# Experts' rows fetched and stored by the DMA queues in place of selection products, and another order of the experts' turns

## The chip, the cores and the metric

One core of a Trainium2 chip runs the whole program once. The metric is the device time of that execution in microseconds (us). PE is TensorE, DVE is VectorE, ACT is ScalarE, POOL is GpSimd, SP is SyncE, whose queue issues the weight loads.

## What is computed

Two blocks of two layers each run over 256 tokens of width 1024, all in float32. The change touches the last half-layer, a mixture of eight SwiGLU experts of which every token uses two:

```python
logits = h @ router_w + router_b                 # 256 x 8
top_vals, top_idx = lax.top_k(logits, 2)
top_w = softmax(top_vals)
combine = sum(one_hot(top_idx, 8) * top_w)       # 256 x 8
y = 0
for e in range(8):
    y = y + combine[:, e:e+1] * ((silu(h @ w_gate[e]) * (h @ w_up[e])) @ w_down[e])
x = x + gate_f * y
return rms_norm(x, final_g)
```

Here h is x normalised, scaled and shifted. An expert's three matrices are 1024 x 3584, 1024 x 3584 and 3584 x 1024.

## The kernel before

The experts stage ends the program. An expert's turn has 14 steps (`ESTEPS`). A step reads 2 MB of gate and up weights (a piece `("gu", s)`) and 1 MB of down weights (`("dn", s)`). SP loads the pieces of all eight turns in one fixed order into 18 units of 1 MB each in SBUF (`LOADS`, `PIECE_AT`); a piece is issued when PE has used what lay in its units (`piece_used`, L775). So at most 18 MB, six steps, are held ahead of PE.

The router's counts decide at run time how wide a turn is (`WIDTHS`, `each_expert`, L619): each engine has one body of code for each width and jumps to it at the head of the turn. In this execution five experts have at most 64 rows (a "few" turn, the body `few(w)`), two have at most 128 (a "full" turn) and one at most 144 (a "wide" turn, `expert_wide`). The wide turn's first step stands apart, in `expert_wide_begin`. Turn 0 is always expert 0; the other seven are sorted by their counts and placed by `RANK_AT`. Before, the turns are few, wide, few, full, few, full, few, few.

What a turn does around its 14 steps:

- **Rows in.** `select` (DVE, L2153) makes the 0/1 matrix `sel` of the next turn's tokens, and PE multiplies the normalised rows `xn` by it: `gather_ahead` (PE, L2935) in three parts at 144 columns, 16 products. ACT (`inputs_ahead`, L1268) and DVE (L2169) scale and shift the result into `hTe`, the next turn's input. This stands at the end of a turn.
- **Rows out.** `by_slot` (PE, L2996) turns the weighted selection `selw`, ACT copies it to `selT`. At the turn's end DVE writes the expert's result rows `ye` (L2228, L2232, L2246), PE multiplies them by `selT` (L3034, L3117), which puts each row at its token's place, and DVE adds the four products to `x` (`add_results`, L2195).

A few turn starts with `gate_up(0)` (L2977), a full turn the same (L2979), the wide one at L3059. A product stands as two records in the trace, a transpose as one. Close to the end of a few or full turn PE runs `gather_ahead(0)`, `turn_hidden(13)`, `gather_ahead(1)`, `down(13)` (L2991, L2993), `gather_ahead(2)` and the scatter L3034.

`addr_align` (L3013, L3093) places two stretches of PE's code at set offsets.

At the program's start SP's first weight load waits for `used[0]`, which POOL gives after its memsets (L864). At the end ACT squares `x`, POOL takes the root (`norm_root_by_rows`), DVE scales and SP stores.

Of the kernel before, what the change touches and what calls it, by code (L numbers as in the profile page):

```python
# [65 lines left out]
AHEAD = WIDTHS[2]  # L66
AHEAD_PARTS = (range(0, 3), range(3, 6), range(6, KD))
# [33 lines left out]
FULL_CLOSE_AT = 74  # L101
WIDE_CLOSE_AT = 16
# [72 lines left out]
RANK_AT = [0] + [(i - 1) // 2 if i % 2 else EXPERTS - 1 - i // 2 for i in range(1, EXPERTS)]  # L175
# [3 lines left out]
def build(nc, t):  # L179
    ctx = ExitStack()  # L180
    with ctx:
# [42 lines left out]
        counts = sb("counts", [P, 2 * EXPERTS], mybir.dt.int32)  # L224

# [127 lines left out]
        selT = ymix[:, 1024:1536].rearrange("p (i s) -> p i s", i=2)  # L353
        ye = rot[:, 2048:4096].rearrange("p (i d) -> p i d", i=2)
# [11 lines left out]
        curp, curw = small[:, 256:258], small[:, 258:260]  # L366
# [88 lines left out]
        route_in = sig("route_in")  # L455
        band_in = sig("band_in")
# [38 lines left out]
        cur_loaded = sig("cur_loaded")  # L495
        sel_ok = sig("sel_ok")
        selw_ok = sig("selw_ok")
# [11 lines left out]
        selT_mm = sig("selT_mm")  # L509
# [8 lines left out]
        stored = sig("stored")  # L518
        out_ok = sig("out_ok")
# [99 lines left out]
        def each_expert(eng, body, begin=None):  # L619
# [7 lines left out]
            with nc.body(f"{name}_head", valid_engines=[eng.engine]):  # L627
# [3 lines left out]
                def run(w, whole=True):  # L631
                    again = eng.mark_branch_hint_location()
                    if whole and begin and w > P:
                        begin(e, w)
                    body(e, w)
                    nc.regs_alu(turn, turn, 1, op=ALU.add)
                    eng.br_lt(turn, EXPERTS, on_true=f"{name}_head", on_false=f"{name}_done{w}").branch_hint(again)
                    with nc.body(f"{name}_done{w}", valid_engines=[eng.engine]):
                        eng.br(f"{name}_end")
# [36 lines left out]
        def few(w):  # L676
            return w == FEW
# [42 lines left out]
        def _(sp):  # L720
# [130 lines left out]
            sp.wait_ge(stored.sem, 16 * NB)  # L851


        @block.gpsimd
        def _(pool):
# [43 lines left out]
            for l in range(DEPTH):  # L899
                norm_root(l * 2)  # L900
                if l == 0:
                    pool.dma_start(route[:], t["route"]).then_inc(route_in.sem, 16)
# [12 lines left out]
            pool.dma_start(rot[:, 2048:4096], t["band"].rearrange("(k p) g s -> p k (g s)", p=P)).then_inc(band_in.sem, 16)  # L915
# [20 lines left out]
            for l in range(DEPTH):  # L936
# [15 lines left out]
                else:  # L952
                    pool.wait_ge(gateB_ok.sem, gateB_ok.at(l, 4))
                    pool.dma_start(finB, t["final_norm_g_2"].partition_broadcast(P)).then_inc(mix_in.sem, 16)
            norm_root_by_rows(U_FIN2)
# [3 lines left out]
        def _(act):  # L959
# [218 lines left out]
            for l in range(DEPTH):  # L1178
# [78 lines left out]
                else:  # L1257
# [10 lines left out]
                    def inputs_ahead(count, bank):  # L1268

                        act.wait_ge(gath_mm.sem, 3 * count - 2)  # L1270
                        for k in AHEAD_PARTS[0]:
                            ins = act.activation(hTe[:, k, 0:AHEAD], bank[:, k * AHEAD:(k + 1) * AHEAD], ACT.Identity, scale=mulc[:, l, 1, k:k + 1], bias=mods[:, l, 3 * KD + k:3 * KD + k + 1])
                        ins.then_inc(hTe_act.sem, 1)
# [18 lines left out]
                    def by_slot(e, w, bank):  # L1292

                        act.wait_ge(selT_mm.sem, e + 1)
                        for i, s0, n in blocks(max(w, P)):
                            ins = act.activation(selT[0:n, i, :], bank[0:n, i * SEQ:(i + 1) * SEQ], ACT.Copy)
                        ins.then_inc(selT_ok.sem, 1)

                    def expert(e, w):

                        last = ESTEPS // 2 - 1
                        if w <= P:
                            act.sem_inc(xTe_act.sem, 1)
                            sigmoids(e, 0, 0, w)
                            by_slot(e, w, T[1])
# [9 lines left out]
                            act.sem_inc(yeT_act.sem, 1)  # L1315
                            return
                        if w > AHEAD:
                            inputs(xgath_mm, e + 1, xTe_act, G[0], AHEAD, w - AHEAD)
                        else:
                            act.sem_inc(xTe_act.sem, 1)  # L1320
# [4 lines left out]
                        by_slot(e, w, S[1])  # L1325
# [7 lines left out]
                        inputs_ahead(e + 2, S[0])  # L1333

                    inputs_ahead(1, G[0])
                    act.wait_ge(counts_ok.sem, 1)
                    each_expert(act, expert)
            act.wait_ge(gath_mm.sem, 3 * (EXPERTS + 1))
            for b in range(NB):
                act.wait_ge(scat_ev.sem, EXPERTS * 4 - 1 + 2 * b)  # L1340
# [4 lines left out]
        def _(dve):  # L1345
# [3 lines left out]
            dve.sem_inc(scat_ev.sem, 1)  # L1349
# [529 lines left out]
            for l in range(DEPTH):  # L1879
# [208 lines left out]
                else:  # L2088
# [4 lines left out]
                    dve.wait_ge(route_in.sem, 16)  # L2093
# [34 lines left out]
                    for b in range(NB):  # L2128
                        ins = dve.tensor_scalar(sel[:, b, :], slots, place[:, b, 0:1], None, ALU.is_equal)
                    ins.then_inc(sel_ok.sem, 1)  # L2130
                    dve.wait_ge(rank_mm.sem, 2)
                    dve.tensor_copy(counts[:, 0:1], S[1][:, 0:1]).then_inc(counts_ok.sem, 1)
                    dve.tensor_copy(curp.unsqueeze(2), place[:, :, 0:1])
                    dve.tensor_copy(curw.unsqueeze(2), weight[:, :, 0:1]).then_inc(cur_loaded.sem, 1)
                    dve.wait_ge(counts_ok.sem, 1)
                    dve.wait_ge(cur_loaded.sem, 1)
# [16 lines left out]
                    def select(e):  # L2153

                        dve.tensor_copy(curp.unsqueeze(2), place[:, :, bass.ds(e, 1)])
                        dve.tensor_copy(curw.unsqueeze(2), weight[:, :, bass.ds(e, 1)]).then_inc(cur_loaded.sem, 1)
                        dve.wait_ge(cur_loaded.sem, e + 1)
                        for b in range(NB):
                            ins = dve.tensor_scalar(sel[:, b, :], slots, curp[:, b:b + 1], None, ALU.is_equal)
                        ins.then_inc(sel_ok.sem, 1)  # L2160

# [7 lines left out]
                    def inputs_ahead(count, part, bank):  # L2169

                        dve.wait_ge(gath_mm.sem, 3 * count - 2 + part)
                        for i, k in enumerate(AHEAD_PARTS[part]):
                            ins = dve.tensor_scalar(hTe[:, k, 0:AHEAD], bank[:, i * AHEAD:(i + 1) * AHEAD], mulc[:, l, 1, k:k + 1], mods[:, l, 3 * KD + k:3 * KD + k + 1], ALU.mult, ALU.add)
                        if part == 2:
                            ins.then_inc(hTe_dve.sem, 1)
# [19 lines left out]
                    def add_results(e, banks):  # L2195

                        dve.wait_ge(scat_ev.sem, e * 4 + 1)
                        for b in range(NB):
                            for half in range(2):
                                j = 2 * b + half  # L2200
                                xs = x[:, b, half * 512:(half + 1) * 512]
                                dve.wait_ge(scat_mm.sem, e * 4 + (j + 1))
                                dve.tensor_tensor(xs, banks[j][:, :], xs, ALU.add).then_inc(scat_ev.sem, 1)

                    def expert(e, w):

                        if w > AHEAD:
                            inputs(xgath_mm, e + 1, xTe_dve, G[1], AHEAD, w - AHEAD)
                        else:
                            dve.sem_inc(xTe_dve.sem, 1)  # L2210

                        n = FEW if few(w) else P * len(blocks(w))
                        for b in range(NB):
                            for c0 in range(0, max(n, P), n):
                                ins = dve.tensor_scalar(selw[:, b, c0:c0 + n], slots[:, 0:n], curp[:, b:b + 1], curw[:, b:b + 1], ALU.is_equal, ALU.mult)
                        ins.then_inc(selw_ok.sem, 1)
                        dve.wait_ge(sel_ok.sem, e + 1)
                        dve.wait_ge(selw_ok.sem, e + 1)
                        select(e + 1)
# [3 lines left out]
                        if w <= P:  # L2223
                            inputs_ahead(e + 2, 1, G[1])
                            dve.wait_ge(down_mm.sem, e * ESTEPS + (FSTEPS + ESTEPS))
                            dve.sem_inc(yeT_dve.sem, 1)
                            if few(w):
# [6 lines left out]
                            inputs_ahead(e + 2, 2, T[1])  # L2234
                            return add_results(e, SCAT)
# [6 lines left out]
                        dve.wait_ge(ye_mm.sem, e + 1)  # L2242
                        for i, s0, n in blocks(w):
# [4 lines left out]
                        inputs_ahead(e + 2, 1, S[1])  # L2248
                        inputs_ahead(e + 2, 2, T[0])
                        add_results(e, G)  # L2250

                    inputs_ahead(1, 1, G[1])
                    inputs_ahead(1, 2, T[1])
                    each_expert(dve, expert)
            dve.wait_ge(scat_ev.sem, EXPERTS * 4 + 1)
# [8 lines left out]
        def _(pe):  # L2264
# [395 lines left out]
            for l in range(DEPTH):  # L2660
# [78 lines left out]
                pe.wait_ge(band_in.sem, 16)  # L2739
# [163 lines left out]
                else:  # L2903
                    pe.wait_ge(route_in.sem, 16)
# [22 lines left out]
                    def gather_wide(w):  # L2927

                        for k in range(KD):
                            for b in range(NB):  # L2930
                                ins = mm(G[k // KH][:, k % KH * P:k % KH * P + w - AHEAD], xn[:, b, k * P:(k + 1) * P], sel[:, b, AHEAD:w], start=(b == 0), stop=(b == NB - 1))
                            if k % KH == KH - 1:
                                ins.then_inc(xgath_mm.sem, 1)

                    def gather_ahead(part, bank):  # L2935
# [320 lines left out]
```

## Time and profile before

| | |
|---|---|
| median of 3 runs | 2415.78 us (2414.87 to 2418.22) |
| the profiled execution | 2413.9 us, span 2412.0 us |
| PE busy | 2370.4 us, 98% of the span |
| DVE, ACT, POOL busy | 935.5, 365.1, 55.4 us |
| chain of work that ended last | PE 92%, DMA 3%, DVE 3% of the span |
| experts stage, first product to the end of the span | 1463.69 to 2412.0 us |
| DMA over the span | 617.59 MB, mean 256 GB/s |

Times of the trace count from the start of the span. The profiled execution's own time is 1.9 us above its span. A busy PE here means that a product is in it, which says nothing of how far it is from its peak.

### The profile page before, as it was taken

How to read it: one execution, taken by the hardware profiler on the slowest of the kernel's cores; microseconds unless marked ns; L12 is line 12 of the kernel's file. 1: busy time of each engine (PE TensorE's matmuls, PEld its weight loads, DVE VectorE, ACT ScalarE, POOL GpSimd, SP SyncE). 2: the span in 40 equal slices, each digit the busy share in tenths (PEclk: the TensorE clock that was granted, in tenths of full speed). 3: DMA queues.
4: the chain of work that ended last, by engine and by line, in shares of the span. 5: the costliest groups of instructions: out<-in, count | busy, mean ns of one | idle time of the engine just before them, and what ended most of it. 6: DMA issues, size and time to landing. Idle time of an engine off the chain costs nothing.

```text
span 2412.0 us, 30124 instructions
## 1 busy us (share of the span) xinstructions
PE 2370.4 (98%) x12002; PEld 1579.7 (65%) x12003; DVE 935.5 (39%) x1962; ACT 365.1 (15%) x988; POOL 55.4 (2%) x110
## 2 busy tenths in 40 slices
PE   9999999999999999999999999999999999999997
PEld 8956476669665666676778756699854455445554
DVE  4565233255563356755687462100211021102111
ACT  2254010012351100011000112100111011101111
POOL 0000000000000000000000000000000000000000
PEclk9999999999999999999999999999999999999999
DMA  7432343444322677554577469974899689968997
GB/s 275 151 113 97 113 170 144 148 180 162 131 78 101 263 299 298 197 199 182 237 297 314 167 234 392 425 292 175 361 417 426 243 343 426 425 270 346 425 426 301
DMA packets 78989, 617.59 MB, mean 256 GB/s; under 512 B 5984, under 2 KB 6112, under 8 KB 39184
## 3 DMA queue, kind: packets, MB, share of 16 engines
q1 hardware_dynamic: 73920, 558.39, 58.3%
q0 software_dynamic: 4656, 56.47, 5.6%
q8 instruction: 98, 1.61, 0.3%
q10 hardware_dynamic: 288, 0.90, 0.1%
q14 instruction: 27, 0.22, 0.0%
HBM read 614.69 MB, written 1.05 MB: 255 GB/s over the span
## 4 chain that ended last, share of the span: by engine, by line
PE 92%; DMA 3%; DVE 3%; ACT 1%; issue 1%; SPq 0%; POOL 0%; DVEq 0%; POOLq 0%; ACTq 0%
PE S L2977 9%; PE T L2597 9%; PE S L2979 8%; PE G L2336 6%; PE G L2613 5%; PE G L2991 4%; PE G L2993 4%; PE G L2368 3%; PE G L2551 3%; PE G L2876 3%; DMA big<-in_moe_pack 3%; PE S L2857 3%; PE T L3045 2%; PE G L2679 2%; PE G L2563 2%; PE G L3072 2%
## 5 line engine op out<-in xcount | busy, mean ns | idle before, releaser
L2191 DVE TENSOR_TENSOR turns<-S,turns 128x128 f32<-128x128 f32 (+2 forms) x105 | 35.5, 338 | 657.4 <-ACT turns L1285 657.4
L2977 PE MATMUL S<-big,hT 128*64 128x256 f32 x2240 | 271.4, 385 | 10.6 <-DMA big<-in_moe_pack 10.5
L2977 PEld LDWEIGHTS S<-big,hT 128*64 128x64 f32 x2240 | 156.9, 138 | 119.1 <-issue 37.0
L2597 PE MATMUL T<-hT,big 128*128 128x256 f32 x960 | 217.2, 379 | 1.1 <-ACT big L1173 1.1
L2597 PEld LDWEIGHTS T<-hT,big 128*128 128x128 f32 x960 | 182.2, 190 | 49.4 <-issue 27.7
L2979 PE MATMUL S<-big,hT 128*128 128x512 f32 x448 | 201.3, 593 | 0.4 <-issue 0.4
L2979 PEld LDWEIGHTS S<-big,hT 128*128 128x128 f32 x448 | 82.8, 190 | 94.8 <-issue 94.8
L2368 PE MATMUL G<-big,hT 128*128 128x384 f32 x320 | 109.0, 490 | 0.8 <-ACT big L1063 0.8
L1290 ACT ACTIVATE pT<-T 128x128 f32<-128x128 f32 (+1 forms) x98 | 30.2, 308 | 521.8 <-PE T L2956 521.8
L2336 PE MATMUL G<-big 128*128 128x186 f32 (+1 forms) x536 | 91.8, 322 | 0.0
L2336 PEld LDWEIGHTS G<-big 128*128 128x128 f32 x536 | 86.6, 190 | 0.2
L2368 PEld LDWEIGHTS G<-big,hT 128*128 128x128 f32 x320 | 59.3, 190 | 40.2 <-issue 4.8
L2991 PE MATMUL G<-big,pT 128*64 128x512 f32 x360 | 84.9, 592 | 0.0
L2551 PE MATMUL G<-big,yT 128*128 128x512 f32 x192 | 83.1, 592 | 0.0
L1794 DVE TENSOR_TENSOR big<-big 128x256 f32<-128x256 f32 x64 | 25.8, 422 | 138.3 <-ACT big L1173 138.2
L2876 PE MATMUL G<-big,pT 128*128 128x512 f32 x176 | 77.4, 593 | 0.8 <-DVE pT L2006 0.7
L1173 ACT ACTIVATE big<-T 128x256 f32<-128x256 f32 x60 | 23.0, 383 | 337.9 <-PE T L2597 337.9
L1424 DVE CUSTOM_DVE_ANT_0 big<-big 128x1024 f32<-128x1024 f32 x64 | 74.1, 1220 | 0.0
L1285 ACT ACTIVATE turns<-S 128x128 f32<-128x128 f32 (+2 forms) x105 | 33.0, 314 | 222.4 <-PE S L2977 93.3
L2551 PEld LDWEIGHTS G<-big,yT 128*128 128x128 f32 x192 | 36.2, 190 | 44.0 <-issue 44.0
L2993 PE MATMUL G<-big,pT 128*128 128x512 f32 x144 | 64.7, 592 | 0.0
L3045 PE MATMUL T<-hT,big 128*128 128x144 f32 x448 | 58.0, 292 | 2.9 <-issue 2.9
(500 smaller groups left out, 3475.5 us busy)
## 6 DMA issues: line engine op xcount, KB each, us to landing
big<-in_moe_pack SPq DMA_DIRECT2D x112, 2048.0 KB, 15.2
big<-in_moe_pack SPq DMA_DIRECT2D x72, 1024.0 KB, 12.4
big<-in_w_ff SPq DMA_DIRECT2D x32, 2048.0 KB, 8.4
big<-in_ada_pack POOLq DMA_DIRECT2D x24, 2048.0 KB, 12.1
big<-in_ffn_pack SPq DMA_DIRECT2D x11, 3072.0 KB, 12.6
big<-in_gate_pack SPq DMA_DIRECT2D x16, 1536.0 KB, 6.4
consts<-in_moe_pack SPq DMA_DIRECT2D x24, 1024.0 KB, 14.3
big<-in_proj_pack SPq DMA_DIRECT2D x15, 1488.0 KB, 6.4
```

What stands on the lines that cost most here:

```text
L1424: ins = dve.tensor_tensor_reduce(row, row, condrow, 1.0, 0.0, ALU.mult, ALU.add, mods[:, a, col:col + 1])
L2336: ins = mm(out, left[:, k, :], right[:, k, :], start=(k == 0 and i not in (2, 3)), stop=(k == KH - 1), skip_group_check=True)
L2368: ins = mm(G[b if n < 4 else 1][:, 0:GATE_N], hT[:, k, b * P:(b + 1) * P], w[:, k, :], start=(k == 0), stop=(k == KD - 1))
L2551: ins = mm(G[j][:, :], yT[:, 4 * n + k, b * P:(b + 1) * P], w[:, k, half * 512:(half + 1) * 512], start=(k == 0), stop=(k == 3))
L2597: ins = mm(up_bank(c, f), w[:, k, f * P:(f + 1) * P], hT[:, k, :], start=(k == 0), stop=(k == KD - 1))
L2613: ins = mm(P7[i][:, :], left[:, f, :], right[:, f, :], start=(c == 0 and f == 0), stop=(c == 7 and f == 1))
L2876: return mm(G[j][:, :], ffhid[:, n % 2, f, b * P:(b + 1) * P], dn[:, f, half * 512:(half + 1) * 512], start=(n == 0 and f == 0), stop=(n = ...
L2977: ins = mm(S[s % 2][f * FEW:(f + 1) * FEW, 0:SEQ], hTe[:, k, 0:FEW], wt[:, k, f * SEQ:(f + 1) * SEQ], start=(k == 0), stop=(k == KD - 1))
L2979: ins = mm(S[s % 2][:, :], hTe[:, k, 0:P], wt[:, k, :], start=(k == 0), stop=(k == KD - 1))
L2991: ins = mm(G[2][half * FEW:(half + 1) * FEW, :], ehid[:, s % 2, f * FEW:(f + 1) * FEW], wt[:, f, half * 512:(half + 1) * 512], start=first ...
L2993: ins = mm(G[2 + half][:, :], ehid[:, s % 2, f * P:(f + 1) * P], wt[:, f, half * 512:(half + 1) * 512], start=first, stop=last)
L3045: ins = mm(H4[2 * (s % 2) + piece][:, f * w:(f + 1) * w], wt[:, k, c0:c0 + P], hTe[:, k, 0:w], start=(k == 0), stop=(k == KD - 1))
```

## The change

Rows in: POOL writes `xn` to a store in DRAM (`row_store`), makes for each turn a list of its tokens in DRAM (four scatters of 128 numbers each), loads the lists (`where`), and fetches for each turn two blocks of up to 128 rows by indirect transfers into `xe`. PE turns a block by eight transposes (`turn_ahead`, `turn_wide`). Only turn 0 is still gathered by products (`gather_first`), at 128 columns. `hTe` ahead of a turn now holds 128 columns, so the wide turn (144) turns its second block in `expert_wide_begin`.

Rows out: a turn's `ye` is stored to `results` in DRAM by two DMAs that ACT issues (`store_results`). Only the last turn still has `by_slot`, the scatter products and `add_results`, now behind the loop (`closing`). During the last turn POOL fetches, for the two token blocks, the earlier and the later result row of each token (four indirect transfers, one after the other), multiplies each by its weight and adds it to `x`.

Further: `results` (8 MB) is filled once, by a POOL DMA in layer 0 of the first block; POOL fills `token_list` ahead of `used[0]`; `RANK_AT` is reversed, which makes the turns few, few, wide, few, full, few, full, few; the two `addr_align` go, one comes at the end of a loop body.

```diff
-AHEAD_PARTS = (range(0, 3), range(3, 6), range(6, KD))
+AHEAD_PARTS = (range(0, KD // 2), range(KD // 2, KD))
-RANK_AT = [0] + [(i - 1) // 2 if i % 2 else EXPERTS - 1 - i // 2 for i in range(1, EXPERTS)]
+RANK_AT = [0] + [TURNS - 1 - (i - 1) // 2 if i % 2 else i // 2 - 1 for i in range(1, EXPERTS)]
...
+            pool.iota(token[:], pattern=[[P, NB]], base=0, channel_multiplier=1)
+            step.do(pool.memset(where[:], 0))
+            pool.dma_start(token_list.rearrange("(p j) o -> p (j o)", p=P), where[:]).then_inc(lists_in.sem, 16)
             for i in range(NSLOT):
                 pool.sem_inc(used[i].sem, 1)
...
+                if l == 0:
+                    pool.wait_ge(consts_in.sem, 16)
+                    pool.dma_start(results.rearrange("s e i (h d) -> s (e i h) d", h=2), vecs[:, V_N - 512:V_N].unsqueeze(1).broadcast_to([P, 2 * LIST, 512])).then_inc(rows_moved.sem, 16)
...
+            def rows_of_turn(e, i):
+                if e + i > 1:
+                    pool.wait_ge(xe_in[i].sem, 16 * (e + i - 1))
+                pool.indirect_dma_start(xe[:, i, :], None, row_store, bass.IndirectOffsetOnAxis(ap=where[:, 2 * e + i:2 * e + i + 1], axis=0)).then_inc(xe_in[i].sem, 16)
...
+            pool.dma_start(row_store.rearrange("(b p) d -> p b d", p=P), xn).then_inc(rows_moved.sem, 16)
+            turn_lists()
+            pool.wait_ge(gath_mm.sem, 2)
+            pool.wait_ge(rows_moved.sem, 48)
+            pool.wait_ge(lists_in.sem, 32 + 64 + 16)
+            rows_of_turn(0, 1)
+            rows_of_turn(1, 0)
+            shares()
+            pool.wait_ge(xgath_mm.sem, 2)
+            rows_of_turn(1, 1)
+            for e in range(2, EXPERTS):
+                pool.wait_ge(gath_mm.sem, 2 * e)
+                rows_of_turn(e, 0)
+                pool.wait_ge(xgath_mm.sem, 2 * e)
+                rows_of_turn(e, 1)
...
+            pool.wait_ge(ye_out.sem, 32 * EXPERTS)
+            rows = results.rearrange("s e i d -> (s e i) d")
+            for n, (b, i) in enumerate(((0, 0), (0, 1), (1, 0), (1, 1))):
+                pool.indirect_dma_start(xe[:, 1, :], None, rows, bass.IndirectOffsetOnAxis(ap=found[:, 2 + i, b:b + 1], axis=0)).then_inc(rows_moved.sem, 16)
+                pool.wait_ge(rows_moved.sem, 16 * (n + 4))
+                w = (w_early, w_late)[i][:, b:b + 1]
+                step.do(pool.tensor_scalar(xe[:, 1, :], xe[:, 1, :], w, None, ALU.mult))
+                ins = pool.tensor_tensor(x[:, b, :], x[:, b, :], xe[:, 1, :], ALU.add)
...
+                    def store_results(e, w):
+                        act.wait_ge(ye_dve.sem, e * 2 + 4)
+                        for i in range(2):
...
+                            act.dma_start(out.rearrange("s e d -> s (e d)"), src).then_inc(ye_out.sem, 16)
...
+                    def turn_ahead(part, bank):
+                        for i, k in enumerate(AHEAD_PARTS[part]):
+                            ins = pe.transpose(bank[:, i * P:(i + 1) * P], xe[:, 0, k * P:(k + 1) * P], ident[:])
+                        ins.then_inc(gath_mm.sem, 1)
...
                         gate_up(e, 0, w)
-                        pe.wait_ge(scat_ev.sem, e * 4 + 1)
-                        by_slot(e, w, T[1])
+                        pe.wait_ge(ye_dve.sem, e * 2 + 2)
                         for s in range(1, ESTEPS):
-                            if s == ESTEPS - 1 and not few(w):
-                                pe.addr_align(FETCHED, offset=FULL_CLOSE_AT, max_nops=0)
                             gate_up(e, s, w)
                             down(e, s - 1, w)
-                        pe.wait_ge(sel_ok.sem, e + 2)
-                        gather_ahead(0, G[0])
+                        pe.wait_ge(xe_in[0].sem, (e + 1) * 16)
+                        turn_ahead(0, G[0])
                         turn_hidden(e, ESTEPS - 1, w)
-                        gather_ahead(1, G[1])
+                        turn_ahead(1, G[1])
                         down(e, ESTEPS - 1, w)
-                        pe.wait_ge(selT_ok.sem, e + 1)
-                        gather_ahead(2, T[1])
```

## Rows read from the trace of the kernel before

**Rows 1.** Windows by turn: stretch, length, busy of each engine, PEclk, DMA share, GB/s.
```profile
1463.70:1550.60 86.90, 84.95 (x617) 45.69 (x617) 16.05 (x50) 10.57 (x34) 0.00 (x0) 1.00 0.98 403
1550.60:1736.50 185.90, 182.97 (x1426) 176.23 (x1426) 21.05 (x47) 17.25 (x28) 0.00 (x0) 0.99 0.73 290
...
1821.60:1977.50 155.90, 155.36 (x408) 71.94 (x408) 20.03 (x47) 13.37 (x33) 0.00 (x0) 1.00 0.80 323
...
2218.50:2303.40 84.90, 84.90 (x619) 45.67 (x620) 14.06 (x45) 10.52 (x33) 0.00 (x0) 1.00 1.01 426
```

**Rows 2.** Windows in the first few turn, columns as in Rows 1.
```profile
1484.00:1550.60 66.60, 64.65 (x464) 34.55 (x460) 11.10 (x31) 8.19 (x25) 0.00 (x0) 1.00 1.01 425
```

**Rows 3.** Timeline, the last turn's last two steps: start, length, engine, line, work.
```profile
2388.81 2.81 PE L2977 MATMUL S<-big,hT 128*64 128x256 f32 x24 [1.58 <-DMA big<-in_moe_pack]
...
2397.79 1.94 PE L2991 MATMUL G<-consts,pT 128*64 128x512 f32 x8
```

**Rows 4.** Timeline, boundary of two few turns.
```profile
2295.11 1.74 PE L2939 MATMUL G<-yT,rot 128*128 128x144 f32 x12
...
2296.99 0.28 ACT L1290 ACTIVATE pT<-T 128x128 f32<-128x128 f32 x1 [3.21 <-PE T L2956]
2297.16 1.19 ACT L1272 ACTIVATE hT<-G,mods,misc 128x144 f32<-128x144 f32 x3
...
2298.36 1.94 PE L2991 MATMUL G<-consts,pT 128*64 128x512 f32 x8
...
2303.32 3.67 PE L2977 MATMUL S<-big,hT 128*64 128x256 f32 x32
```

**Rows 5.** Timeline, the wide turn: its second step, its end, the turn behind it.
```profile
1563.27 8.79 PE L3045 MATMUL T<-hT,big 128*128 128x144 f32 x56 [2.93 <-issue]
...
1720.86 0.73 PE L3096 MATMUL G<-zcol,consts 128*128 128x2 f32 x6
...
1723.55 1.06 PE L3107 MATMUL T<-consts,hT 128*128 128x128 f32 x8
...
1725.53 1.29 DVE L2246 TENSOR_TENSOR rot<-T,o 128x512 f32<-128x512 f32 x2 [3.30 <-PE G L3107]
...
1736.48 3.67 PE L2977 MATMUL S<-big,hT 128*64 128x256 f32 x32
```

**Rows 6.** Timeline, boundary of a full and a few turn.
```profile
1965.58 1.63 PE L2939 MATMUL G<-yT,rot 128*128 128x144 f32 x12
...
1968.74 3.60 PE L2993 MATMUL G<-consts,pT 128*128 128x512 f32 x8
...
1977.46 3.67 PE L2977 MATMUL S<-big,hT 128*64 128x256 f32 x32
```

**Rows 7.** Timeline, start of the program.
```profile
1.18 0.42 SPq L724 DMA_DIRECT2D big<-in_proj_pack  x1
...
7.91 6.49 PE L2296 MATMUL G<-big,hT 128*128 128x372 f32 x20 [0.16 <-DMA big<-in_proj_pack]
```

**Rows 8.** Timeline of POOL: a DMA's issue and two small operations.
```profile
18.95 0.71 POOL L902 DMA_DIRECT2D route<-in_route  x1
...
113.25 0.23 POOL L874 TENSOR_TENSOR small<-small,epsc 128x20 f32<-128x20 f32 x1
...
1441.70 0.19 POOL L874 TENSOR_TENSOR small<-small,epsc 128x1 f32<-128x1 f32 x1 [14.47 <-ACT pT L969]
```

**Rows 9.** A window in layer 0 of the first block, columns as in Rows 1.
```profile
340.00:360.00 20.00, 20.00 (x75) 13.86 (x74) 4.15 (x7) 1.15 (x3) 0.00 (x0) 1.00 0.44 161
```

**Rows 10.** Timeline, the gather of turn 0 and its first products.
```profile
1458.00 4.61 PE L2939 MATMUL G<-yT,rot 128*128 128x144 f32 x24
...
1463.69 3.67 PE L2977 MATMUL S<-big,hT 128*64 128x256 f32 x32
```

**Rows 11.** DMA issues, 1390 to 1463 us: size, median us from issue to landing.
```profile
yT<-in_final_norm_g POOLq DMA_DIRECT2D x1, 512.0 KB, 11.4
```

**Rows 12.** DMA issues, 2290 to 2412 us.
```profile
big<-in_moe_pack SPq DMA_DIRECT2D x11, 2048.0 KB, 32.3
```

More of the change, by code:

```diff
@@ L100 @@
 FETCHED = 256
[L101 to L102 removed]
+REST_AT = 100
 KH = KD // 2
@@ L518, in build @@
         stored = sig("stored")
+        xe_in = [sig(f"xe_in{i}") for i in range(2)]
+        ye_out = sig("ye_out")
         out_ok = sig("out_ok")
@@ L638, in run @@
                     with nc.body(f"{name}_done{w}", valid_engines=[eng.engine]):
+                        if closing:
+                            closing(w)
+                        if begin and w == P:
+                            eng.addr_align(FETCHED, offset=REST_AT, max_nops=0)
                         eng.br(f"{name}_end")
@@ L1290, in hidden_turned, with by_slot @@
                         act.activation(ehid[:, i, 0:n], T[0][:, i * SEQ:i * SEQ + n], ACT.Copy).then_inc(eh_ok.sem, 1)
[L1292 to L1296, printed above, removed]
-                        ins.then_inc(selT_ok.sem, 1)
+                    def by_slot(w):
+                        act.wait_ge(scat_mm.sem, 1)
+                        if few(w):
+                            ins = act.activation(selTN, T[1][:, 0:SEQ], ACT.Copy)
+                        else:
+                            for i, s0, n in blocks(w):
+                                ins = act.activation(selT[0:n, i, :], (T[1] if w <= P else G[0])[0:n, i * SEQ:(i + 1) * SEQ], ACT.Copy)
+                        ins.then_inc(selT_ok.sem, 1)
+                    def store_results(e, w):
+                        act.wait_ge(ye_dve.sem, e * 2 + 4)
+                        for i in range(2):
+                            h = slice(i * 512, (i + 1) * 512)
+                            if few(w):
+                                out, src = results[0:FEW, bass.ds(e, 1), 0, h], ye[i * FEW:(i + 1) * FEW, 0, 0:512]
+                            elif w <= P:
+                                out, src = results[:, bass.ds(e, 1), 0, h], ye[:, 0, h]
+                            else:
+                                n = blocks(w)[i][2]
+                                out, src = results[0:n, bass.ds(e, 1), i, :], ye[0:n, i, :]
+                            act.dma_start(out.rearrange("s e d -> s (e d)"), src).then_inc(ye_out.sem, 16)
                     def expert(e, w):
@@ L3098, in expert_wide @@
                         pe.sem_inc(eh_turned.sem, ESTEPS)
[L3099 to L3102 removed]
+                        pe.wait_ge(xe_in[0].sem, (e + 1) * 16)
+                        turn_ahead(0, S[0])
                         pe.wait_ge(yeT_act.sem, e + 1)
@@ L3108, in expert_wide @@
                         ins.then_inc(ye_mm.sem, 1)
[L3109 to L3118 removed]
+                        turn_ahead(1, S[1])
                     def any_expert(e, w):
```

267 lines of the change are left out of this document (155 added, 112 removed).

## The prediction

> **What bounds the kernel now.** I first cut the experts stage into its turns [rows 1]. PE is busy through each turn, so every record that leaves PE shortens a turn unless the weights are late. The GB/s column says when they are: a few turn draws 403 to 426 GB/s with a DMA share near 1, a full or wide one 290 to 323. A turn reads 42 MB of weights. At 425 GB/s [rows 2] a unit of 1 MB (1.049e6 bytes) takes 2.47 us and a turn's 42 units 103.6 us. A few turn is shorter than that and lives on the 18 units held ahead; full and wide turns fill them again. Two few turns in a row outrun the loads: in the last turn PE waits for weights, 1.58 us before step 13 [rows 3], and its last `down` ends at 2399.73, 96.4 us into the turn against 81.8 us one turn earlier [rows 3, 4]. So 14.6 us of the last pair is weights. Then I read what PE does between the last steps of a turn and the first products of the next [rows 4 to 6], because the change removes most of it.
>
> **The change part by part.** All sums are against the profiled execution (span 2412.0, time 2413.9), 1.9 below the median 2415.78.
>
> *Start.* SP's first load, issued at 1.18, is what PE's first product waits for [rows 7]. POOL now runs an iota, a memset and a DMA issue ahead of its release. The issue is 0.71, small operations about 0.2 each [rows 8], with their waits **+1.3** (0.9 to 2.5; the iota isn't in the trace, the nearest row is 0.2).
>
> *Filling `results`.* 8.4 MB in layer 0 of the first block. There DMA moves 161 GB/s [rows 9], so 264 are free and it takes 32 us under products that wait for nothing: 0. With no cover it would be 8.4/0.425 = 20 us.
>
> *Turn 0's gather.* 32 records at 128 columns for 32 at 144 (5.7 us to the first product [rows 10]): **-0.7**.
>
> *A few turn's boundary.* From `gather_ahead(0)` to the next `gate_up(0)`: 2295.11 to 2303.32, 8.2 us [rows 4]. After: four transposes 0.5 (eight are 1.06 [rows 5]), `turn_hidden` 0.3, four transposes 0.5, 0.1 for ACT's copy (0.28), `down` 1.94. ACT's four scalings (three are 1.19) and VectorE's four end under `down`. The jump to the next body, which the scatter products covered, gets 0.4 more. In all 3.7, saved 4.5; with the two transposes and the wait of `by_slot` in step 1 (0.5) **-5.0** a turn. Queued behind the new wait for `xe_in` is all of PE; rows are asked for a whole turn ahead, so I charge nothing. For turn 1 they come last: lists by some 28 small POOL operations (0.3 each with their waits, 8 us), then three DMA rounds of 0.7 plus 11.4 each [rows 8, 11]; begun at about turn 0's first product, that ends near 1508, and they are due some 75 us into the turn, near 1540. If they were late by 20 us, it would cost nothing either, since that turn pair waits for weights.
>
> *A full turn's boundary.* 1965.58 to 1977.46, 11.9 [rows 6], becomes 0.5 + 0.3 + 0.5 + 0.3 + 3.6 = 5.2; with `by_slot` **-7.1** a turn.
>
> *The wide turn's.* 1720.86 to 1736.48, 15.6 [rows 5]. After: 0.7, 0.5, a wait of 0.9 for the copies, sixteen transposes 2.1, four more 0.5, then VectorE's four `ye` operations (1.29 for two) and four scalings before the second half of `gate_up(0)`, 2.4 net. In all 7.1, **-8.5**. At its start `turn_wide` (1.1) and a second block of scalings, behind ACT's stores, come new: **+4.0**.
>
> *ACT's stores.* Two issues a turn, 0.4 each by the nearest row [rows 7], between `ye` and the first sigmoid, 3.7 us after the turn's start [rows 4]: hidden, with 1 us to spare beside the table load. Each further us would move PE by as much, a turn.
>
> *The order.* The pair of few turns now stands at the front. Weights decide it again. From the pair's start to its last `gate_up` took 2388.81 - 2218.5 = 170.3. The first pair begins with all 18 units landed; I credit one unit, -2.5. New traffic shares the stretch: five blocks of 0.5 MB, turn 0's results (0.26 MB), lists, the tail of `row_store`: 2.9 MB at 425 GB/s is 6.8, with small pieces **+8** (5 to 28: at the upper end each block holds the loads for half of its 11.4). So 175.8, then step 13 and the boundary, 10.9 before and 9.1 after. The saved boundaries of these two turns are lost to the weights. Behind the pair the wide turn refills all units, and no other pair is left.
>
> *Tail.* ACT now copies the turned selection after the last turn's two stores, and PE waits for it: **+3.0** (1 to 6).
>
> The sum, first product to last `down`. Before: 1463.7 to 2399.7, 936.0. After: pair 184.9, wide start 4.0, wide 177.4, few 79.9, full 148.8, few 79.9, full 148.8, last few 79.5, in all 903.2. That is -32.8; with +1.3, -0.7 and +3.0, **-29.2**: 2384.7 for the profiled execution, 2386.6 on the median's scale. I say **2386**.
>
> *The results' fetch* hides under the last few turn and has little cover to spare. It begins when turn 6's stores have landed (0.9 + 0.8 + 11.4 = 13.1). Four times a fetch (0.7 + 11.4) and two POOL operations on 1024 columns follow; by the slope of 20 columns against one [rows 8], 2.1 ns a column, that is 2.3 each. 13.1 + 4 x 16.7 = 80. It is due at 79.5 + 3.4 = 83. I take 0, the last fetches being quicker once the weights have landed. Lower end 0; upper end 32.3 a fetch, the big pieces' landing in the last turns [rows 12]: 13.1 + 4 x 37.6 = 163, 80 late.
>
> The Trainium skill ("DMA: Bandwidth & Descriptors", section "Anatomy of one DMA — SWDGE (gpsimd) path") gives such a DMA about 2.0 us plus its bytes at 436 GB/s, an estimate of 3.2 for half a MB. The row of 11.4, taken while the weights ran at full rate, differs. By the page the chain would end at 47 and the late cases below would fall away; the sum would stay.
>
> **The rivals.**
>
> *The pair costs more.* The new transfers slow the weights beyond their bytes. For it: 11.4 for half a MB. Against it: the traffic kept its 425 GB/s [rows 2]. At the upper end +20, 2406.
>
> *Code late at the boundaries.* The wide turn's second step began after 2.93 us in which PE waited for nothing that the profile shows, behind a jump [rows 5]. The `addr_align` go, every body moves, and the products that covered the jump are gone. At all seven boundaries that is 20: 2406. Against it: the few and full boundaries of before show no such gap [rows 4, 6].
>
> *The results' fetch is late, and still faster.* Landings of 12 to 19 us: 2387 to 2414. A rule puts a mechanism of its own here: POOL held while VectorE works. VectorE is busy 14.06 us of a few turn [rows 1]; if POOL lost all of it in the last turn, the chain would end at 94, 11 late: 2397. The Trainium skill ("SBUF — State Buffer", section "SBUF: two separate sides") states it as an exclusive lock on a shared port that keeps POOL from writing descriptors. The trace of before can't show it, since POOL does nothing during the turns [rows 1].
>
> *Slower.* The same four fetches, one behind the other: each us of landing counts four times. The change loses from 11.4 + (3 + 29)/4 = 19.4 us a fetch on; at 32.3 the program ends at 2386 + 80 = 2466. For it: the fetches run against weights that land after 32. Against it: they are of another queue, and the one POOL row is 11.4.
>
> **How the numbers follow.** Within 0.2% (5 us) a measurement of this kernel can't be told from no change. Forecast 0.52 (own range 2372 to 2396); pair dearer 0.09; code late 0.11; fetch late but faster 0.14, the lock 0.04 of it; fetch late and slower 0.10; all gains lost to several of these, no change, 0.04. So faster 0.86, same 0.04, slower 0.10. The range takes the forecast's lower end with its smallest costs (start 0.9, pair 5, tail 1, jumps 0: 2386 - 0.4 - 3 - 2 - 3, and a fuller start of the pair, 8 more), 2368, up to 2412, which leaves out the slower case and the far end of the late one: **2368 to 2412**.
>
> **What would show it.** Right: few turns near 80 and full ones near 149 us in the windows by turn; the waits for `moe_pack` in the second turn, none in the last; no scatter products but four at the end; POOL's last addition to `x` before the last `down`. Wrong: PE or VectorE waiting for POOL at the end; gaps of 2 to 3 us in front of the first `gate_up`; ACT's sigmoid late behind its DMA issues; first products later than 1464.3; PE waiting for `xe` at the end of turn 0 beyond what the weights would have cost.

## The result, and the profile after

The changed kernel takes 2401.9 us (median of 5 runs, 2400.4 to 2404.3) against 2415.8 before (median of 5): a ratio of 0.994, 95% interval 0.9929 to 0.9951. It is 13.9 us faster, where 29.8 were forecast: inside the range of 2368 to 2412, with half of the gain. The profiled execution has a span of 2398.6 us, where the forecast's sum gives 2412.0 - 29.2 = 2382.8.

The windows by turn answer to [rows 1]; the turns are now few, few, wide, few, full, few, full, few. Columns: stretch, its length, busy time of PE, its weight load, DVE, ACT and POOL with their instructions, PEclk, DMA share, GB/s. The third line is the wide turn; the stretch above it also holds the wide turn's start, and the last one ends with the last `down`.

```profile
1463.90:1543.70 79.80, 79.27 (x583) 41.72 (x582) 11.10 (x37) 10.31 (x33) 19.06 (x45) 1.00 1.01 416
1543.70:1654.50 110.80, 87.29 (x591) 46.90 (x591) 11.61 (x38) 13.08 (x39) 2.61 (x3) 0.95 1.01 426
1654.50:1826.80 172.30, 170.43 (x1382) 169.96 (x1382) 15.19 (x32) 16.84 (x27) 0.94 (x1) 0.99 0.77 312
1826.80:1908.30 81.50, 79.75 (x583) 41.97 (x583) 12.12 (x39) 10.43 (x33) 2.20 (x3) 1.00 1.01 424
1908.30:2057.00 148.70, 148.57 (x374) 67.04 (x374) 13.35 (x33) 13.40 (x33) 2.48 (x3) 1.00 0.88 362
2057.00:2145.70 88.70, 81.97 (x583) 43.89 (x583) 11.37 (x35) 10.43 (x33) 1.24 (x2) 0.98 1.01 425
2145.70:2294.40 148.70, 148.57 (x372) 67.07 (x372) 13.41 (x33) 13.40 (x33) 1.23 (x2) 1.00 0.87 360
2294.40:2383.50 89.10, 81.91 (x584) 43.58 (x584) 10.82 (x34) 10.44 (x33) 24.82 (x12) 0.98 0.95 397
```

Beside the forecast's own terms:

| stretch | forecast | measured | difference |
|---|---|---|---|
| first few pair, to its last `down` (1648.07) | 184.9 | 184.2 | -0.7 |
| wide start (to 1654.49) | 4.0 | 6.4 | +2.4 |
| wide turn | 177.4 | 172.3 | -5.1 |
| few turn 3 | 79.9 | 81.5 | +1.6 |
| full turn 4 | 148.8 | 148.7 | -0.1 |
| few turn 5 | 79.9 | 88.7 | +8.8 |
| full turn 6 | 148.8 | 148.7 | -0.1 |
| few turn 7, to its last `down` | 79.5 | 89.1 | +9.6 |
| sum | 903.2 | 919.6 | +16.4 |

The program reaches the first product 0.4 earlier than forecast (1463.9) and its tail is 0.2 shorter (2383.5 to 2398.6, 15.1). So the missing 16 us lie in the turns: turns 5 and 7 lost 18.4, and the other stretches together gained 2.0. Turn 0 took 79.8 us with the same work; turns 5 and 7 took 9 us more each. The chain of what ended last, and the waits of PE over the experts stage (us in total, times, longest), say to what:

```profile
PE 87%; DMA 7%; DVE 3%; ACT 1%; SPq 1%; issue 1%; ACTq 0%; POOL 0%; DVEq 0%; POOLq 0%
```

```profile
PE S L3095 <- DMA big<-in_moe_pack: 31.9, 18, 4.2
PE S L3188 <- ACT hT L1386: 5.1, 1, 5.1
PE G L3154 <- ACT yT L1417: 2.6, 1, 2.6
PE S L3097 <- DMA big<-in_moe_pack: 1.8, 2, 0.9
```

Before, the chain had 3% of DMA, and PE's waits for `moe_pack` were 10.5 us, all in the last pair. Now they are 33.7 us. Why a few turn behind a full one waits at all, though a full turn has time to refill the units, is seen on SP's queue. This is its timeline in full turn 4 (start, length, queue and line, tile; a group reaches from its first to its last issue), and the windows there, columns as above:

```profile
1975.24 21.95 SPq L787 DMA_DIRECT2D big<-in_moe_pack  x5
1997.45 0.33 SPq L787 DMA_DIRECT2D turns<-in_moe_pack  x1
2020.78 0.33 SPq L787 DMA_DIRECT2D consts<-in_moe_pack  x1
2027.86 21.36 SPq L787 DMA_DIRECT2D big<-in_moe_pack  x10
```

```profile
2000.00:2010.00 10.00, 10.00 (x26) 4.45 (x26) 0.85 (x2) 0.77 (x2) 0.00 (x0) 1.00 0.78 332
2010.00:2020.00 10.00, 10.00 (x26) 4.45 (x25) 0.85 (x2) 0.77 (x2) 0.00 (x0) 1.00 0.00 0
2020.00:2030.00 10.00, 10.00 (x26) 4.54 (x25) 0.85 (x2) 0.77 (x2) 0.00 (x0) 1.00 0.44 134
2030.00:2040.00 10.00, 10.00 (x26) 4.54 (x25) 0.85 (x2) 0.77 (x2) 0.00 (x0) 1.00 1.00 403
```

SP's waits for PE in that stretch, 1990 to 2050 (us in total, times, longest):

```profile
SPq L787 <- PE G L3111: 27.9, 3, 22.7
SPq L787 <- PE S L3097: 23.9, 4, 6.6
```

The loads stand in one queue. The piece `("dn", 13)` (in `consts`, unit 16) may be loaded only when PE has used `("dn", 9)`, which lies in the same unit. SP waits 22.7 us for that (for L3111, the full turn's `down`), and DMA moves nothing from 2010 to 2020. The next turn's `("gu", 0)` stands behind it, and it has a wait of its own: its units 0 and 1 hold `("gu", 11)` until PE has used that (L3097, the full turn's `gate_up`), 6.6 us more. So two places set the restart, and a free place for `("dn", 13)` alone would not have moved it. `("gu", 0)` goes out at 2027.86, 29.2 us before the full turn ends. At 425 GB/s 11.8 units can land in that time, where the forecast had all 18 full. From there DMA is busy throughout (share 1.00, 416 GB/s) to the end of turn 5, 117.8 us after that load. PE's last wait for weights in turn 5 ends at 2135.93. Up to there DMA moved 414 GB/s for 108.1 us, 42.7 units: the turn's pieces up to that one are 40, the new transfers of the stretch 1.5, and later pieces were under way. In turn 7 it is the same: 2265.31 to 2383.48, 118.2.

The kernel before had the same standstill. SP's timeline of before, full turn 3, not among the rows ahead of the prediction:

```profile
1934.36 0.33 SPq L773 DMA_DIRECT2D consts<-in_moe_pack  x1
1941.44 21.36 SPq L773 DMA_DIRECT2D big<-in_moe_pack  x10
```

There the load of `("gu", 0)` came 36.0 us before the full turn's end (1977.46), and the few turn behind it ended at 2062.60, 121.2 us after the load, without a wait. The change takes 7.1 off the full turn's end and 5.0 off the few turn. Both lie inside this stretch: 121.2 - 12.1 = 109.1 was what the forecast asked for, 117.8 is what it took with the weights as the limit. The difference, 8.7, is what turn 5 lost.

### The profile page after: what moved, and what is told of

Read it like the earlier page. It is cut to its first block, busy times and chain, and to the rows that moved or that the text cites. A ratio compares the mean times of both kernels' runs of the same rounds, so it can differ in the third digit from the quotient of the medians.

```text
span 2398.6 us, 29590 instructions
## 1 busy us (share of the span) xinstructions
PE 2327.4 (97%) x11738; PEld 1550.4 (65%) x11739; DVE 899.8 (38%) x1869; ACT 367.8 (15%) x994; POOL 115.7 (5%) x194
## 4 chain that ended last, share of the span: by engine, by line
PE 87%; DMA 7%; DVE 3%; ACT 1%; SPq 1%; issue 1%; ACTq 0%; POOL 0%; DVEq 0%; POOLq 0%
PE T L2710 9%; PE S L3097 8%; PE S L3095 7%; DMA big<-in_moe_pack 7%; PE G L2449 6%; PE G L2726 5%; PE G L3111 4%; PE G L2481 4%; PE G L2664 3%; PE G L3109 3%; PE G L2989 3%; PE S L2970 3%; PE G L2792 2%; PE T L3174 2%; PE G L2676 2%; PE G L3201 2%
## 5 line engine op out<-in xcount | busy, mean ns | idle before, releaser
L3095 PE MATMUL S<-big,hT 128*64 128x256 f32 x2240 | 276.5, 391 | 34.0 <-DMA big<-in_moe_pack 31.9
L3095 PEld LDWEIGHTS S<-big,hT 128*64 128x64 f32 x2240 | 163.1, 140 | 144.1 <-issue 65.4
L3097 PE MATMUL S<-big,hT 128*128 128x512 f32 x448 | 201.0, 593 | 1.8 <-DMA big<-in_moe_pack 1.8
L3097 PEld LDWEIGHTS S<-big,hT 128*128 128x128 f32 x448 | 82.9, 190 | 97.3 <-issue 93.7
L3111 PE MATMUL G<-big,pT 128*128 128x512 f32 x144 | 64.7, 592 | 0.0
L2989 PEld LDWEIGHTS G<-big,pT 128*128 128x128 f32 x176 | 32.7, 190 | 38.7 <-issue 37.3
```

Of the source, the lines that this page charges most:

```text
L2989: return mm(G[j][:, :], ffhid[:, n % 2, f, b * P:(b + 1) * P], dn[:, f, half * 512:(half + 1) * 512], start=(n == 0 and f == 0), stop=(n = ...
L3095: ins = mm(S[s % 2][f * FEW:(f + 1) * FEW, 0:SEQ], hTe[:, k, 0:FEW], wt[:, k, f * SEQ:(f + 1) * SEQ], start=(k == 0), stop=(k == KD - 1))
L3097: ins = mm(S[s % 2][:, :], hTe[:, k, 0:P], wt[:, k, :], start=(k == 0), stop=(k == KD - 1))
L3111: ins = mm(G[2 + half][:, :], ehid[:, s % 2, f * P:(f + 1) * P], wt[:, f, half * 512:(half + 1) * 512], start=first, stop=last)
```

## Experiments

Three theories, as the expectations number them. Theory 1: the place of the pieces makes the loads restart late, and the few turns behind a full turn are bound by weights. Theory 2: the new transfers on the queues of POOL and ACT slow the weights beyond their bytes. Theory 3: the new order of the turns is what costs. The first four kernels ran beside runs of before with a median of 2416.3 us, the other four beside 2416.6.

### The same kernel, other places for the later pieces

The first twelve pieces stay; thirteen of the others move to units that come free earlier. `("dn", 13)` now has to wait for `("dn", 4)` in place of `("dn", 9)`, and the next turn's `("gu", 0)` for `("gu", 6)` in place of `("gu", 11)`.

```diff
-GU_AT = (0, 2, 5, 8, 11, 14, 0, 2, 6, 8, 11, 0, 4, 14)
-DN_AT = (4, 7, 10, 13, 16, 17, 5, 10, 13, 16, 2, 7, 17, 16)
+GU_AT = (0, 2, 5, 8, 11, 14, 0, 3, 8, 12, 6, 4, 8, 13)
+DN_AT = (4, 7, 10, 13, 16, 17, 2, 10, 15, 11, 17, 10, 15, 16)
```

> The changed kernel, with only the places of the later weight pieces in the 18 units changed, so that no load has to wait for a piece that is used late while other units are free. Theory 1 (the few turns behind a full turn are bound by weights, because the loads stand still 15 to 17 us in each full turn and start again too late): the waits for weights of turns 3, 5 and 7 go (1.6 + 8.7 + 9.5 = 19.8 us above the forecast), the first pair costs some 2 us more; 2384 us, 2380 to 2389; turns 5 and 7 take 80 to 81 us and 80 to 81 us. Theory 2 (the new small transfers on the POOL and ACT queues slow the weights beside them): the bytes and their places in time are nearly the same, so 2398 to 2404 us, turn 5 over 86 us. Theory 3 (the new order of the turns costs it): no change, 2399 to 2405 us.

Measured: 2383.3 us (2381.9 to 2385.7), ratio to before 0.9862 (0.9847 to 0.9877). Its windows for turns 3, 4, 5 and 7, and SP's timeline in full turn 4:

```profile
1828.30:1908.70 80.40, 79.51 (x583) 41.65 (x583) 11.97 (x39) 10.45 (x33) 2.08 (x3) 1.00 1.00 411
1908.70:2057.40 148.70, 148.57 (x372) 67.05 (x372) 13.51 (x33) 13.44 (x33) 2.61 (x3) 1.00 0.91 376
2057.40:2137.50 80.10, 79.32 (x584) 41.77 (x583) 11.26 (x35) 10.46 (x33) 1.08 (x2) 1.00 1.01 422
...
2286.20:2366.40 80.20, 79.56 (x584) 42.09 (x584) 10.81 (x34) 10.46 (x33) 24.88 (x12) 1.00 0.94 394
```

```profile
1996.72 14.29 SPq L787 DMA_DIRECT2D big<-in_moe_pack  x4
2011.32 0.33 SPq L787 DMA_DIRECT2D consts<-in_moe_pack  x1
2012.01 41.08 SPq L787 DMA_DIRECT2D big<-in_moe_pack  x10
```

`("gu", 0)` now goes out at 2012.01, 45.4 us ahead of the full turn's end in place of 29.2, and the few turns take the forecast's 80. Theory 1 holds with its number, and this is the fastest kernel here that computes everything. All transfers, their bytes and the order of the turns are as they were, so theories 2 and 3 are not needed for these 18.6 us. The edit moves more than the restart; that the restart is what counts is read from SP's timeline, and from DMA, which in the changed kernel had no pause left in turn 5 that another place could have filled. The pair at the front waits as before: 185.1 us to its last `down`.

### Most of the new transfers taken away

```diff
-                rows_of_turn(e, 1)
+                if e == 2:
+                    rows_of_turn(e, 1)
+                else:
+                    pool.wait_ge(xe_in[1].sem, 16 * e)
+                    pool.dma_start(xe[0:1, 1, 0:SEQ], row_store[0:1, 0:SEQ]).then_inc(xe_in[1].sem, 16)
...
-                            act.dma_start(out.rearrange("s e d -> s (e d)"), src).then_inc(ye_out.sem, 16)
+                            act.dma_start(out.rearrange("s e d -> s (e d)")[0:1], src[0:1]).then_inc(ye_out.sem, 16)
```

> The changed kernel without most of its new transfers: each turn's result stores carry one row instead of all, and the second block of rows is fetched in the turns 0, 1 and 2 alone, with one row of 1 KB in its place in the others (so the output lacks the results of the turns before the last). Some 0.75 MB less in a few turn and 1 MB in a full one. Theory 1 (weights, bytes alone): at 425 GB/s 2.3 us off each of turns 5 and 7, 1.6 off turn 3, 2 to 3.5 off the first pair; 2392 us, 2388 to 2397. Theory 2 (the transfers slow the weights beyond their bytes): the waits of turns 3, 5 and 7 go altogether, some 20 us, and more of the pair's; 2376 to 2384 us. Theory 3 (the order): within 3 us of 2402.

Measured: 2394.3 us (2393.5 to 2395.6), ratio 0.9908 (0.9892 to 0.9923); inside theory 1's range, far from theory 2's. Turn 5:

```profile
2054.10:2139.00 84.90, 79.98 (x583) 42.41 (x582) 11.36 (x35) 10.44 (x33) 1.21 (x2) 1.00 1.01 426
```

It is 3.8 us shorter than in the changed kernel and still 4.8 longer than with the new places. A full turn's results (0.5 MB) and one second block of rows (0.5 MB) are gone from the stretch that binds it, 2.5 us at 425 GB/s; 2.3 was expected. PE's busy time fell by 2.0 (81.97 to 79.98): some products of turn 5 that ran slowly in the changed kernel (last section) do not here. Turn 7 gained only 0.4. In its stretch no row block is fetched in either kernel, so only turn 6's results are gone: 1.2 us by their bytes, not the 2.3 expected. So the new transfers cost about their bytes, and not the 20 us of theory 2.

### The order alone, and the rows alone

The kernel before with the new `RANK_AT`:

```diff
-RANK_AT = [0] + [(i - 1) // 2 if i % 2 else EXPERTS - 1 - i // 2 for i in range(1, EXPERTS)]
+RANK_AT = [0] + [TURNS - 1 - (i - 1) // 2 if i % 2 else i // 2 - 1 for i in range(1, EXPERTS)]
```

> The kernel before with the new order of the turns and nothing else. Theory 1: in the kernel before a few turn takes 85 us, just longer than the weights behind a full turn need, so the order moves only the pair from the end to the start; the end pair's 10.5 us of waits for weights go, 5 to 10 come back in turn 1; 2411 us, 2407 to 2416. Theory 2: the same, there are no new transfers. Theory 3 (the order costs 15 us or more in itself): 2425 to 2435 us.

The changed kernel with the line of before (the same diff the other way round):

> The changed kernel with the order of the turns of the kernel before (few, wide, few, full, few, full, few, few). Theory 1: the few turns behind the full ones wait for weights as they do now, and the last few turn, the second of a pair at the end, waits 15 to 25 us; 2408 us, 2403 to 2415. Theory 3 (the order takes what the rows gain): 2384 to 2392 us. Theory 2 says the same as theory 1 within its bounds.

Measured: the order alone 2412.4 us, ratio 0.9986 (0.9977 to 0.9995); the rows alone 2404.2, ratio 0.9947 (0.9934 to 0.9961). With the order alone the pair takes 178.0 us to its last `down`, against 181.3 at the end of the kernel before, and few turns 3 and 5 keep 85.1. Rows alone, the turns 4, 6 and 7 (windows):

```profile
1953.00:2040.70 87.70, 80.36 (x583) 42.83 (x582) 11.35 (x35) 10.44 (x33) 1.16 (x2) 1.00 1.01 424
...
2189.40:2278.50 89.10, 80.43 (x583) 42.83 (x582) 11.34 (x35) 10.44 (x33) 0.59 (x1) 1.00 1.01 424
2278.50:2386.70 108.20, 87.77 (x583) 46.66 (x584) 9.69 (x33) 10.44 (x33) 24.81 (x12) 0.94 0.94 397
```

The few turns behind a full one are as long as in the changed kernel, whatever the order. Theory 3 falls: the order gains some 2 to 4 us in either kernel and loses none. Both times lie inside theory 1's ranges.

### The new places in the kernel before, and with the old order

The diff of the first experiment, on the kernel before and on the kernel "rows alone":

> The kernel before with the same new places of the weight pieces and nothing else. Theory 1 (the limit behind a full turn lies just under the 85 us that a few turn takes in the kernel before, and the change went below it): turns 4 and 6 of this kernel wait for nothing and gain nothing, only the pair at the end gains, by up to 6 us; 2411 us, 2407 to 2417. Rival (the places were poor in any case, and the 18 us have nothing to do with the change): 2394 to 2400 us.

> The changed kernel with the new places of the weight pieces and with the order of the turns of the kernel before. Theory 1 (the order only moves the pair): turns 2, 4 and 6 at 80 to 81 us, and the pair at the end waits as long as the one at the start, some 25 us, with the 2 MB of the last fetches beside it up to 5 more; 2386 us, 2381 to 2391. Theory 3 (the order itself costs): 2365 to 2375 us.

Measured: on before 2413.7 us, ratio 0.999 (0.9981 to 0.9999); with the rows and the old order 2386.2, ratio 0.9871 (0.9856 to 0.9886). So the same two lines are worth 0.1% in the kernel before and 0.8% in the changed one. That is 2.9 us before (2416.6 to 2413.7) and 18.6 after. In the kernel before, a few turn behind a full one takes 85.1 us with either map: the restart was early enough for it. The end pair gained less than the 6 us allowed for (180.8 in place of 181.3). With the old order the few turn behind a full one is 80.4 us, and the pair at the end waits as expected:

```profile
2181.10:2261.50 80.40, 79.50 (x583) 41.96 (x582) 11.35 (x35) 10.45 (x33) 0.59 (x1) 1.00 1.01 424
2261.50:2369.70 108.20, 86.78 (x583) 46.30 (x583) 9.69 (x33) 10.46 (x33) 24.83 (x12) 0.95 0.94 397
```

### Half of the down weights left where they are

```diff
-                c0, n = (0, 2 * UNIT) if kind == "gu" else (2 * UNIT, UNIT)
-                sp.dma_start(unit_rows(LOADS[m]), t["moe_pack"][e, s][:, c0:c0 + n]).then_inc(arrival(PIECES.index(LOADS[m]))[0], 16)
+                c0, n = (0, 2 * UNIT) if kind == "gu" else (2 * UNIT, UNIT // 2)
+                sp.dma_start(unit_rows(LOADS[m])[:, 0:n], t["moe_pack"][e, s][:, c0:c0 + n]).then_inc(arrival(PIECES.index(LOADS[m]))[0], 16)
```

> The changed kernel with only the first half of each down piece loaded from the second expert on (half of the down weights are old ones, so the output differs): 35 MB a turn in place of 42. Theory 1: no turn waits for weights, also not the first pair; the 33.7 us of such waits go and nothing comes in their place; 2368 us, 2364 to 2373, every few turn near 80 us. Rival (a few turn cannot take 80 us behind a full one for another reason, POOL's fetches or the row transposes): turns 5 and 7 stay over 84 us, 2376 us or more.

Measured: 2360.1 us (2359.8 to 2360.9), ratio 0.9764 (0.9749 to 0.9779). Turn 1 with the wide start, turns 5 and 7:

```profile
1543.60:1633.10 89.50, 81.70 (x590) 44.07 (x590) 11.63 (x38) 13.07 (x39) 2.61 (x3) 0.99 1.01 421
...
2035.80:2115.90 80.10, 79.34 (x584) 41.75 (x583) 11.26 (x35) 10.45 (x33) 1.16 (x2) 1.00 1.01 419
...
2264.60:2343.90 79.30, 79.28 (x584) 41.83 (x584) 10.83 (x34) 10.45 (x33) 24.84 (x12) 1.00 0.86 357
```

The rows, the transposes and the fetches are all there, and a few turn takes 80 us: nothing but weights kept it longer. The time is below the expected range (2364 to 2373): the gain of 41.8 is 8 us above the 33.7 of waits, so the expectation, which had nothing beside the waits, was too small. From the first product to the last `down` it is 880.4 in place of 919.6. PE's waits for weights fell by 31.2 (2.5 are left), and its busy time by 877.75 - 868.30 = 9.5 with the same products: some had run slowly behind the waits. The last section shows one.

### Without the results' stores

This is for the 5.1 us at the wide turn's start, where PE waits for ACT.

```diff
-                            act.dma_start(out.rearrange("s e d -> s (e d)"), src).then_inc(ye_out.sem, 16)
+                            act.sem_inc(ye_out.sem, 16)
```

> The changed kernel without the results' stores: ACT raises the semaphore in their place (so the output lacks the results of the turns before the last). This is for the 5.1 us that PE waits at the wide turn's start. Theory 1 (ACT's two DMA issues and the code around them stand ahead of the scalings of the wide turn's second block): the wait falls to 1 to 2 us. Rival (the jump to the wide body and the table load cost it): it stays over 4 us. In all, with the stores' bytes gone too, 2395 us by the first (2391 to 2398), 2398 by the rival.

Measured: 2394.1 us (2391.9 to 2395.2), ratio 0.9902 (0.9887 to 0.9917); but the wait is still 4.0 us. First the changed kernel, then this one (timeline, ACT and PE at the wide start):

```profile
1649.24 1.17 ACTq L1435 DMA_DIRECT2D results<-rot  x2
...
1651.83 1.28 ACT L1386 ACT_TABLE_LOAD   x1 [4.45 <-issue]
1653.12 1.13 ACT L1386 ACTIVATE hT<-G,mods,misc 128x16 f32<-128x16 f32 x4
```

```profile
1648.21 1.09 PE L3056 MATMUL G<-consts,rot 128*128 128x128 f32 x8 [0.27 <-issue]
...
1650.65 1.28 ACT L1386 ACT_TABLE_LOAD   x1 [3.40 <-issue]
1651.95 1.13 ACT L1386 ACTIVATE hT<-G,mods,misc 128x16 f32<-128x16 f32 x4
...
1653.32 2.12 PE L3188 MATMUL S<-hT,big 128*128 128x144 f32 x8 [4.02 <-ACT hT L1386]
```

The stores cost 1.1 us there, so my theory fell, and the wait agrees with the rival (it stays over 4 us). The total does not part the two (2395 and 2398 were expected): the stores' bytes are gone as well. The rows show what PE's 4.0 us are made of. PE's `turn_wide` (L3056) ends at 1649.30; then come 1.35 us in which ACT waits for nothing that the profile shows, a table load of 1.28 and the scalings. They are not the wide body's own: in the changed kernel 1.3 to 1.4 us lie between ACT's DMA issues and the table load at the few and full boundaries too, where PE does not wait for them. What fills them stays open, so the jump is not shown as a cause.

## Why the prediction was right and wrong

**Wrong: the weights behind a full turn.** The step that failed is "full and wide turns fill them again", and on it "Behind the pair the wide turn refills all units, and no other pair is left", with its sums of 79.9 and 79.5 for turns 3, 5 and 7, which put the wait for weights behind a full turn at nothing. It took the mean rate of a full turn, 323 GB/s [rows 1], as a sign that the 18 units are full at its end. They are not: 29.2 us of loads are some 12 units. The loads stand still, for two places in the buffer, and restart at a set point of the turn. From there a few turn behind it ended 117.8 and 118.2 us after `("gu", 0)` went out, with DMA busy (shares 1.00 and 0.95). The kernel before used 121.2, so 3.4 of the 12.1 us saved in each full turn and the few turn behind it could be kept. Twice 8.7 is 17.4 of the loss; turns 5 and 7 show 18.4, the last with the fetches' 2 MB beside its weights. Turn 3, behind the wide turn, lost 1.6 (80.4 with the new places). Against the forecast the three turns lost 20.0 us; the first experiment gives 18.6 of it back by moving the restart, and the same edit gives 2.9 before the change. Loading half of the down weights takes the wait away too. That cause is shown.

**Right in its size: the boundaries.** Full turns 148.7 for 148.8; turn 0 79.8 for 79.9. Where weights don't bind, a few turn takes 79.3 to 80.4. The row transposes cost PE what was charged, and it nowhere waits for rows.

**Right: the pair.** 184.2 for 184.9. The 8 us of new traffic and 2.5 of credit were both estimates, and the runs bear both out. The order alone, without new traffic, took 178.0 where the pair at the end took 181.3: a credit of 3.3. From 178.0 to 184.2, with the last step and boundary 2.0 shorter (8.9 for 10.9), the traffic cost 8.2. Half the down weights show that some 21 us of its length (turn 1: 104.4 to 83.2 to the last `down`) is weights, the slow products behind the waits included.

**Right in sum: start, gather and tail.** First product 1463.9 for 1464.3, but in part by luck: the program's first weight product began 0.4 us later and not 1.3 (8.33 for 7.91, outside the 0.9 to 2.5), and turn 0's gather took 0.3 less and not 0.7. Tail 15.1 for 15.3. In the tail PE waits 2.6 us for ACT, behind ACT's two DMA issues (1.18); without stores that wait is 1.4.

**Off in both directions: the wide turn.** Its start took 6.4 for 4.0 (no table load and none of ACT's time ahead of it were charged). The turn itself took 13.6 off for 8.5: its boundary went from 15.6 [rows 5] to 5.5 (1821.27 to 1826.77), 1.6 more than forecast, the gap of 2.93 in its second step [rows 5] did not return, and 0.6 more is not traced.

**The rivals.** Three of them would have given times near the measured one, and none is what happened. The pair was not dearer. No few or full boundary shows code late by 2 to 3 us; they show 0.5 at most. ACT's open 1.3 to 1.4 us may be of that kind; PE pays for them at the wide boundary alone. One sign of being wrong did show: in turn 5 ACT's first sigmoid began 5.2 us into the turn and not 3.7 (2062.19), behind its DMA issues, those open 1.3 us and the table load, but PE did not wait for it. The results' fetch was hidden: this is POOL's first and last round in turn 7, and PE's last `down`.

```profile
2310.45 1.00 POOL L1066 DMA_INDIRECT rot<-results,idx  x1 [18.87 <-DMA results<-rot]
2322.61 2.85 POOL L1069 TENSOR_SCALAR rot<-rot,small 128x1024 f32<-128x1024 f32 x1 [11.17 <-DMA rot<-results,idx]
...
2359.29 1.01 POOL L1066 DMA_INDIRECT rot<-results,idx  x1 [0.27 <-POOL x L1070]
2368.81 2.84 POOL L1069 TENSOR_SCALAR rot<-rot,small 128x1024 f32<-128x1024 f32 x1 [8.51 <-DMA rot<-results,idx]
2371.74 2.35 POOL L1070 TENSOR_TENSOR x<-x,rot 128x1024 f32<-128x1024 f32 x1
...
2381.54 1.94 PE L3109 MATMUL G<-consts,pT 128*64 128x512 f32 x8
```

The chain ends at 2374.1, 9.4 us before the last `down` and 79.7 into the turn, where the sum of its terms gave 80. VectorE was busy for 10.8 us of this turn. POOL lost nothing of that size: its two operations took 2.8 and 2.4 us in each of the four rounds. With the new places of the weights the last turn is shorter, and the spare falls to 1.6 us (POOL ends at 2364.7, the last `down` at 2366.4). A longer fetch chain was not tried, so what a late one would cost is untested. (The lower end of the range is 2369.6 by its own terms; 2368 stands there.)

## What to carry to other kernels

When loads stand in one ordered queue in front of a buffer, read from the queue's own timeline where they last stood still, and take the time from that restart to the end of the work it feeds as a floor; a mean rate below the maximum does not say that the buffer is full. All savings that lie between one restart and that end share the same few us of spare, so they are not to be added turn by turn. Places in the buffer that cost next to nothing (0.1% before) can be the bound after a change that makes the work shorter (0.8%), so the map is to be looked at again after it.

## What the runs showed of the hardware

A wait for weights can cost PE more than its length. In turn 5 of the changed kernel (timeline, PE):

```profile
2113.40 2.81 PE L3095 MATMUL S<-big,hT 128*64 128x256 f32 x24 [1.58 <-DMA big<-in_moe_pack]
...
2121.17 4.50 PE L3095 MATMUL S<-big,hT 128*64 128x256 f32 x24 [1.97 <-DMA big<-in_moe_pack]
...
2128.57 2.81 PE L3095 MATMUL S<-big,hT 128*64 128x256 f32 x24
```

Behind the third wait in three steps (0.72, 1.58, 1.97 us) the same 24 products took 4.50 us in place of 2.81. The granted clock in two windows of 4 us there is 0.69 and 0.88, a mixture of 2.4 and 1.2 GHz, and 1.00 on both sides (columns as above):

```profile
2120.00:2124.00 4.00, 2.83 (x16) 2.08 (x18) 0.00 (x0) 0.00 (x0) 0.00 (x0) 0.69 1.06 449
2124.00:2128.00 4.00, 4.00 (x27) 2.11 (x25) 0.58 (x2) 0.55 (x2) 0.00 (x0) 0.88 0.97 408
```

The next step did not wait, so the loads caught up part of it meanwhile. Not every wait does this. In turn 1 four waits of 1.6 us in successive steps left the 24 products at 2.81 us; behind waits of 4.24 and 4.07 us they took 4.50 and 5.39.

The four indirect fetches of results, 128 rows of 4 KB each, took 8.4 to 11.2 us behind their issue (1.0) in turn 7, where DMA moved 397 GB/s in all; the row fetches of the turns took a median of 12.9 us from issue to landing. The estimate by the Trainium skill ("DMA: Bandwidth & Descriptors", section "Anatomy of one DMA — SWDGE (gpsimd) path") is 3.2 us for such a fetch; these rows differ, as the one row of before did.
